# Two units of an output projection and two of a feed-forward stage in token halves, without GpSimd

## The reference, cut to what matters

```python
x = x + rms_norm_2(merged @ w_out[l], norm_mix_post_g[l])   # output projection, its norm, residual
h = rms_norm_2(x, norm_ffn_pre_g[l])                        # norm ahead of the third FFN
f = (jax.nn.silu(h @ w_gate[l]) * (h @ w_up[l])) @ w_down[l]
x = x + rms_norm_2(f, norm_ffn_post_g[l])
```

## Time and profile before

| what | us |
|---|---|
| median of 3 runs | 1896.39 |
| the three runs | 1894.55, 1896.39, 7628.95 |
| the profiled execution | 1894.26 |
| its span, first to last instruction | 1892.5 |
| TensorE busy | 1870.1 (99%) |
| VectorE, ScalarE, GpSimd busy | 926.3 (49%), 717.8 (38%), 164.4 (9%) |
| granted TensorE clock, mean over the span | 0.997 of full |

### The profile page before, as it was taken

The page is one execution under the profiler, slowest core; times in us unless marked ns, Lnnn a source line. Parts: engine busy times, 40 slices in busy tenths (PEclk is TensorE's granted clock), DMA queues, the critical chain, the costliest instruction groups (busy, mean ns, idle before and its releaser), DMA issues.

```text
span 1892.5 us, 23419 instructions
## 1 busy us (share of the span) xinstructions
PE 1870.1 (99%) x9226; PEld 1527.5 (81%) x9226; DVE 926.3 (49%) x1202; ACT 717.8 (38%) x973; POOL 164.4 (9%) x141
## 2 busy tenths in 40 slices
PE   9999999999999999999999999999999899999998
PEld 7888888887779888888888888777888778888887
DVE  4444431456685655544443146654666364444323
ACT  6223222364534443432232134445664452232222
POOL 0000000125330200200000012110100030000000
PEclk9999999999999999999999999999999999999999
DMA  6343332232214223333332224333422323433322
GB/s 179 89 109 90 90 110 89 101 100 91 68 47 154 89 90 100 101 89 95 104 89 97 103 69 135 114 100 95 126 78 90 89 67 89 110 89 91 109 89 78
DMA packets 214304, 184.15 MB, mean 97 GB/s; under 512 B 7685, under 2 KB 192090, under 8 KB 214234
## 3 DMA queue, kind: packets, MB, share of 16 engines
q1 hardware_dynamic: 213536, 183.13, 31.8%
q10 hardware_dynamic: 698, 0.05, 0.0%
HBM read 172.67 MB, written 2.10 MB: 92 GB/s over the span
## 4 chain that ended last, share of the span: by engine, by line
PE 94%; DVE 3%; ACT 1%; issue 1%; POOL 0%; DMA 0%; SPq 0%; DVEq 0%; ACTq 0%
PE bank L545 26%; PE bank L547 26%; PE bank L546 26%; PE bank L725 6%; PE bank L593 2%; PE bank L595 2%; PE bank L594 2%; PE bank L1023 1%; DVE n_lo L1648 1%; PE bank L1007 1%; ACT w_hi L1123 1%; PE bank L993 1%; PE bank L992 0%; DVE x L2184 0%; PE bank L609 0%
## 5 line engine op out<-in xcount | busy, mean ns | idle before, releaser
L1639 DVE TENSOR_TENSOR w_lo<-w_raw,w_hi 128x2048 fp32r<-128x2048 f32 x160 | 368.2, 2301 | 716.4 <-ACT w_hi L1123 716.2
L545 PE MATMUL bank<-n_hi,w_hi 128*128 128x512 f32 x1760 | 702.2, 399 | 11.0 <-DVE n_lo L1648 9.7
L547 PE MATMUL bank<-n_hi,w_lo 128*128 128x512 f32 x1760 | 687.1, 390 | 0.0
L546 PE MATMUL bank<-n_lo,w_hi 128*128 128x512 f32 x1760 | 686.8, 390 | 0.0
L1123 ACT CAST w_hi<-w_raw 128x2048 fp32r<-128x2048 f32 x160 | 305.5, 1909 | 601.6 <-PE bank L547 508.6
L545 PEld LDWEIGHTS bank<-n_hi,w_hi 128*128 128x128 f32 x1760 | 331.1, 188 | 84.0 <-issue 11.5
L547 PEld LDWEIGHTS bank<-n_hi,w_lo 128*128 128x128 f32 x1760 | 330.9, 188 | 70.1
L546 PEld LDWEIGHTS bank<-n_lo,w_hi 128*128 128x128 f32 x1760 | 331.4, 188 | 68.3 <-issue 3.4
L481 POOL TENSOR_TENSOR sum_squares<-sum_squares,sq 128x512 f32<-128x512 f32 x35 | 61.6, 1760 | 900.2 <-ACT sq L1138 896.9
L545 PE MATMUL bank<-h_hi,w_hi 128*128 (+1 forms) x352 | 137.2, 390 | 0.2
L547 PE MATMUL bank<-h_hi,w_lo 128*128 (+1 forms) x352 | 136.9, 389 | 0.0
(11 more groups left out here) (302 smaller groups left out, 1828.8 us busy)
## 6 DMA issues: line engine op xcount, KB each, us to landing
w_raw<-in_w_in SPq DMA_DIRECT2D x68, 512.0 KB, 4.6
w_raw<-in_ffn_down SPq DMA_DIRECT2D x44, 512.0 KB, 4.0
w_raw<-in_ffn_gate SPq DMA_DIRECT2D x43, 512.0 KB, 4.0
w_raw<-in_ffn_up SPq DMA_DIRECT2D x43, 512.0 KB, 5.2
w_raw<-in_w_gate SPq DMA_DIRECT2D x22, 512.0 KB, 4.0
w_raw<-in_w_up SPq DMA_DIRECT2D x22, 512.0 KB, 5.2
w_raw<-in_w_down SPq DMA_DIRECT2D x22, 512.0 KB, 3.9
w_raw<-in_w_kv_mem SPq DMA_DIRECT2D x16, 512.0 KB, 4.5
```

Of the source, the lines that this page charges most:

```text
L545: pe.matmul(acc, w_hi, x_hi, start=start, stop=False)
L546: pe.matmul(acc, w_hi, x_lo, start=False, stop=False)
L547: return pe.matmul(acc, w_lo, x_hi, start=False, stop=stop)
L1639: dve.tensor_tensor(wlo[par][:, :], raw[par][:, :], whi[par][:, :].bitcast(F32), ALU.subtract).then_inc(w_lo_ready, 1)
```

## The change

Five things are done.

1. U_OUT2+2 and U_OUT2+3 are each done in two passes over 256 of the 512 tokens (`dense_half`): first half of unit 2, first half of unit 3 (banks 0 to 3), then second half of unit 2 and of unit 3 (banks 4 to 7). The sum over partitions and the root are done for each half (`sum_post`, `post_root`).
2. The first two units of the third FFN are done in token halves (`half_units`): both units on the first 256 tokens, then both on the second. The sums and turns hang in between as hooks.
3. `tmp`, `x`, `n_hi` and `n_lo` of this stage are made in halves of 256 tokens.
4. GpSimd does nothing more there: its products go to VectorE, and so do its sums of squares, which VectorE now adds after the second half from a new tile `lastsq` (8 chunks; it lies over tiles that are free at that time).
5. The preload of ScalarE's table ahead of the last root falls away, and the first two copies of turned tokens (`copy_turned`) come ahead of unit 2's cast.

The core of the diff, PE first, then ScalarE, then VectorE:

```diff
-            pool.wait_ge(rstd_ready, R_POST2 + 1)
-            for c in range(1, C, 2):
...
-            add_squares(S_FFN3, range(3, C))
+            def dense_half(u, first_bank, half, xh, xl, hooks=None):
+                unit_split(u)
+                s = u % 2
+                for m in range(2):
+                    for k in range(C):
+                        w0 = k * 256 + m * P
+                        mm = products(bank[first_bank + m][:, HALF[0]], whi[s][:, w0:w0 + P], wlo[s][:, w0:w0 + P],
+                                      xh[:, k, HALF[half]], xl[:, k, HALF[half]], k == 0, k == C - 1)
+                        if k == C - 1:
+                            mm.then_inc(unit_done if m and half else half_done, 1)
+                        if hooks and C * m + k in hooks:
+                            hooks[C * m + k]()
+                def half_units():
+                    hooks = {(0, 0, 1): lambda: sum_post(1), (0, 1, 4): turn_first, (1, 1, 2): sum_last, (1, 1, 6): turn_rest}
+                    for half in range(2):
+                        for jj in range(2):
+                            u = base + jj
+                            par = u % 2
+                            unit_split(u)
+                            for k in range(C):
+                                if jj == 0:
+                                    pe.wait_ge(n_ready, C * index + half_count(half, k))
+                                for g in range(2):
+                                    w0 = (g * C + k) * P
+                                    mm = products(bank[2 * jj + g][:, HALF[half]], whi[par][:, w0:w0 + P],
+                                                  wlo[par][:, w0:w0 + P], nhi[:, k, HALF[half]], nlo[:, k, HALF[half]],
+                                                  k == 0, k == C - 1)
...
+            def sum_post(half):
+                pe.wait_ge(sq_added, post_add(C - 2, half))
+                acc = bank[4 * half][:, HALF[0]]
+                pe.matmul(acc, ones[:, :], sumsq[:, HALF[half]], start=True, stop=False)
+                pe.wait_ge(sq_ready, post_square(C - 1, half))
+                pe.matmul(acc, ones[:, :], sq[(C - 1) % 2][:, HALF[half]], start=False, stop=True).then_inc(sq_summed, 1)
+            for j in (2, 3):
+                dense_half(U_OUT2 + j, 2 * j, 1, mhi, mlo, {2: lambda: sum_post(0)} if j == 2 else None)
...
+            for c in range(4, C):
+                post_chunk(c, 0)
+            post_root(0)
+            post_chunk(4, 1)
+            for c in range(3):
+                last_hi(c, 0)
+            split_unit(U_FFN3)
+            post_chunk(5, 1)
+            for c in (3, 4):
+                last_hi(c, 0)
+            post_chunk(6, 1)
+            last_hi(5, 0)
+            post_chunk(7, 1)
+            split_unit(U_FFN3 + 1)
+            last_hi(6, 0)
+            last_hi(7, 0)
+            post_root(1)
+            for c in range(C):
+                last_hi(c, 1)
+                act.activation(lastsq[:, c, :], x[:, c, :], ACT.Square).then_inc(sq_ready, 1)
+            act.wait_ge(xt_turned, 2)
+            for i in range(2):
+                copy_turned(i, x_tok_a)
             split_unit(U_FFN3 + 2)
-            inverse_root(S_FFN3, R_FFN3)
...
+            def post_half(half, between):
+                cols = HALF[half]
+                dve.wait_ge(rstd_ready, R_POST2 + half + 1)
+                post_scaled(0, half)
+                for c in range(C):
+                    if c < C - 1:
+                        post_scaled(c + 1, half)
+                    dve.wait_ge(scaled, half_count(half, c))
+                    dve.tensor_tensor(x[:, c, cols], tmp[c % 2][:, cols], x[:, c, cols], ALU.add).then_inc(x_ready, 1)
+                    if c:
+                        last_lo(c - 1, half)
+                    between(c)
+                last_lo(C - 1, half)
+            def between_first(c):
+                if c == 1:
+                    post_sum(4, 1)
+                if c == 3:
+                    split_unit(U_FFN3)
+                    post_sum(5, 1)
+                if c == 5:
+                    post_sum(6, 1)
...
+            for c in (4, 5, 6):
+                post_sum(c, 0)
+            post_half(0, between_first)
             split_unit(U_FFN3 + 1)
+            post_half(1, lambda c: None)
+            for c in range(1, C):
...
+                dve.tensor_tensor(sumsq[:, :], lastsq[:, 0, :] if c == 1 else sumsq[:, :], lastsq[:, c, :], ALU.add).then_inc(sq_added, 1)
             ffn_steps(2, U_FFN3, R_FFN3)
```

More of the change, by code:

```diff
@@ L645, in gate_up, with turn_first, sum_last, turn_rest @@
                             hooks[k]()
-                def turn_middle():
-                    pe.wait_ge(rstd_ready, R_FFN3 + 1)
[L649 to L654, removed]
+                def turn_first():
+                    pe.wait_ge(rstd_ready, R_POST2B + 1)
+                    turn_x(0, 4)
+                    turn_x(1, 6)
+                def sum_last():
+                    pe.wait_ge(xt_ready, 4)
+                    pe.wait_ge(sq_added, last_add(C - 1))
+                    pe.matmul(bank[7][:, :], ones[:, :], sumsq[:, :], start=True, stop=True).then_inc(sq_summed, 1)
+                def turn_rest():
+                    pe.wait_ge(rstd_ready, R_FFN3 + 1)
+                    turn_x(2, 4)
+                    turn_x(3, 6)
+                def half_units():
[13 more added lines that the diff above has]
+                                                  k == 0, k == C - 1)
+                                if half and k == C - 1:
+                                    mm.then_inc(unit_done, 1)
+                                if (half, jj, k) in hooks:
+                                    hooks[half, jj, k]()
                 if f == 0:
@@ L1167, in inverse_root, with copy_turned @@
                 act.activation(rstd[:, :], sumsq[:, :], ACT.Exp, scale=-0.5).then_inc(rstd_ready, 1)
+            def copy_turned(i, dst):
+                for half in range(2):
+                    act.copy(dst[:, i % 2, T * half:T * half + T],
+                             bank[4 + 2 * (i % 2) + half][:, :]).then_inc(xt_ready, 1)
             def ffn_steps(f, base):
@@ L1186, in gate_up @@
                     act.copy(dst, tmp[jj][:, :]).then_inc(h_hi_ready, 1)
[L1188 to L1191, removed]
                 b = base + 2
                 if f == 2:
-                    act.wait_ge(xt_turned, 1)
-                    copy_turned(0, x_tok_a)
+                    inverse_root(S_FFN3, R_FFN3, load=False)
                 for j in range(2):
@@ L1609, in _, with post_chunk @@
-            inverse_root(S_POST2, R_POST2, 6, load=False)
-            feed(N_FFN3, X_MIX2, "norm_ffn_pre_g_2", S_FFN3, U_FFN3 + 1, lag=3)
+            def post_chunk(c, half=None):
+                if half is None:
+                    act.wait_ge(unit_done, U_OUT2 + c // 2 + 1)
+                    b, cols, src = c, slice(0, T), slice(0, T)
+                else:
+                    if half and c % 2:
+                        act.wait_ge(unit_done, U_OUT2 + c // 2 + 1)
+                    else:
+                        act.wait_ge(half_done, c - 3 if not half else 5 + (c - 4) // 2)
+                    b, cols, src = c if half else c - 4, HALF[half], HALF[0]
+                if c >= 3:
+                    act.wait_ge(sq_added, post_add(c - 2, half if half and c >= 6 else 0))
+                dst = (sq[c % 2] if c else sumsq)[:, cols]
+                act.activation(dst, bank[b][:, src], ACT.Square, scale=0.5).then_inc(sq_ready, 1)
+                act.activation(ypost[:, c, cols], bank[b][:, src], ACT.Copy, scale=small[:, PG + c:PG + c + 1]).then_inc(ypost_ready, 1)
@@ new lines, in _ @@
+            for j in range(2):
+                split_unit(U_OUT2 + j + 2)
+                for c in (2 * j, 2 * j + 1):
+                    post_chunk(c)
+            for c in range(4, C):
[10 more added lines that the diff above has]
+            last_hi(5, 0)
@@ L2166, in _ @@
             split_unit(U_OUT2 + 1)
[L2168 to L2186, removed]
```

90 lines of the change are left out of this document (54 added, 36 removed).

## The result

| | median us | runs | ratio to before, fast runs (95%) |
|---|---|---|---|
| before | 1894.75 | 5 (1894.29 up, one of 7628.95) | |
| changed | 1885.02 | 5 (1883.09 to 1886.40) | 0.9945 (0.9932 to 0.9959) |
| changed, again | 1883.71 | 5 (1883.38 to 1885.37) | 0.9939 (0.9925 to 0.9952) |

The ratio is that of the fast executions, and the one of 7628.95 us is not among them. The profiled execution took 1883.09 us with a span of 1881.3.

A forecast was written before the change was run, and what follows sets the result against it. TensorE bounds, busy 1870.1 of 1892.5 us. In the stage 46.0 + 1.7 + 0.9 + 3.5 + 0.9 = 53.0 for 63.4, -10.4; 1883.9 or 1886.0 by starting run, taken as 1885.2; range 1881.5 to 1891.5.

The forecast's parts named there:

- Half-width matmuls: Four units' 192 matmuls become 384 of 256 columns at 0.1198 us: 46.0 against 43.5, +2.5 us on TensorE's path.
- The order on TensorE: U_OUT2+2 to FFN unit 2, laid out in time: waits of 0.4 and 0.5 us, end at 1537.8, -10.4 us.
- GpSimd taken out: VectorE takes about 8 us more work, but its instructions lose 7 us of excess; covered by TensorE's second halves.
- The clock: TensorE's low clock from 1514.85 to 1520.83 goes, as no wait exceeds 0.5 us: 2.8 us back, inside the sum.
- Rival 1: VectorE's first pass is slower than said: gain only 3 to 8 us, 1886 to 1893; chance 0.15.
- Rival 2: Weight loads of 0.192 us set the pace of half-width matmuls: +30 instead of +2.5, end at 1913; chance 0.03.
- Rival 3: The clock falls in another place where a wait grows: price 2.8 us, 1888 or more; chance 0.04.
- Rival 4: More gain: no new waits, half-width starts exactly half of 0.2267 apart; 13.8 us at most, 1882.4; chance 0.06.
- Rival 5: GpSimd's work lay under waits the halves remove anyway; time stays near 1885; no chance of its own given.

The follow-up runs named there:

- e4: Kernel before with the 20 gate units in the third FFN's loop done in two passes of 256 tokens; 1909.57 us, ratio 1.0072.
- e2: Kernel before, full width, with GpSimd's products and adds of the stage moved to VectorE; stage 60.11 us, median 1890.92 us, ratio 0.9978.
- e3: Changed kernel plus a chain of eleven GpSimd multiplies of 128x512 on a scratch tile; stage 61.70 us, median 1892.14 us, ratio 0.9982.
- e7: Changed kernel plus one 128x512 VectorE instruction after each chunk of VectorE's second pass (4.8 us more); stage 56.87 us, ratio 0.9968.
- e1: Kernel before plus 50 matmuls on constants between the post sum and the third FFN; stage 64.3 us, median 1895.12 us, ratio 1.0000.
- e6: Changed kernel plus one 128x512 VectorE instruction after each chunk of VectorE's first pass (4.8 us more); stage 55.68 us, ratio 0.9954.
- e8: Changed kernel with the second half's sum and the first two turns moved to other places on TensorE; stage 52.27 us, median 1883.13 us, ratio 0.9931.
- e9: Changed kernel with the output projection back to full width and only the FFN's two units in halves; stage 58.83 us, ratio 0.9970.
- e10: Kernel before plus 25 matmuls on constants ahead of the third FFN; stage 64.3 us, median 1895.59 us, ratio 1.0004.
- the last version: Changed kernel with two hooks moved on TensorE, run again beside the changed kernel; stage 52.25 us, median 1882.52 us, ratio 0.9930.

## Why the prediction was right

Forecast: 1885.2 us, 10.4 us in the stage, against 1885.02 (1883.71 the second time) and 10.3. Point by point:

- *Half-width matmuls.* 0.1198 was taken from the memory keys; the stage shows 0.1199 and the loop of e4 0.12 over 1920 of them. The term of 2.5 us holds. One reading beside it was wrong. Solving the two spacings (0.1198 for 256 columns, 0.2267 for 512) gives a fixed part of 0.013 us a matmul; the 6 ns named in the prediction are what a half-width matmul costs over half a full one. By the formula of the Trainium skill ("TensorE: Matmul & The Clock Gate", Back-to-back issue gap) e4 would have cost an estimated 2.5 us; it cost 13.6, so the measurement decides. The same section of the Trainium skill says that the formula is for matmuls apart from a stream of weight loads, and that within such a stream it is too low for small ones and too high for large ones. The trace agrees for 256 columns (0.1198 us against 0.109) but not for 512 (0.2267 against 0.216).
- *The order on TensorE.* The waits were to be 0.4 and 0.5, for the second sum and for `w_lo`. The list of waits has only 0.34 for `w_lo`, but the starts show both: 0.43 us ahead of the second sum where 0.12 is normal, with another 0.1 inside it, and 0.62 ahead of 1515.41. The stage is 1.0 us longer than its work (53.10 against 52.1) where 0.9 was forecast. Unit 2 at 1537.8 forecast, measured 1537.10 with a start 0.79 earlier: 0.1 us off. VectorE's passes end at 1513.1 and 1524.5, where 1513.8 and 1525.1 were forecast: 0.7 earlier, nearly that shift.
- *GpSimd taken out.* The reason was right: the long instructions were contention (e2, e3), and VectorE could carry the work. The prediction counts 12 half products as new; they stand for four full ones of 0.60 dropped and 16 half ones of 0.34 added, so the new work was reckoned at 7.2 us and not 8, which the forecast does not use. The adds were mis-sized: 0.80 apart, not 0.60, which cost nothing in the changed kernel and showed only in e7.
- *The clock.* Here the account was right as an account and wrong as a cause. I counted 13.8 us in which TensorE did not work at full pace, and 2.8 of them as the low clock's. That the clock stays up in the changed kernel came true. But e1 shows that lifting the clock alone gives nothing in the kernel before, because the low parts of the chunks set the pace. The 2.8 us come back only because the halves take away the wait in which they lay.
- *The rivals.* Rival 1 (VectorE's first pass) did not occur, but e6 shows that it is where the risk was: 4.8 us more on VectorE cost 2.6. Rival 2 fell with e4. Rival 3, a low clock in another place, did not occur in the changed kernel, but e3 shows its kind: after a wait of 6.5 us the low clock cost 2.0 to 2.8 us, near the price of 2.8. Rival 4's kind of gain exists, 0.8 us, by moving the hooks (e8); its figure of 1882.4 follows from no starting point given there (1885.2 less the further 3.4 is 1881.8). Rival 5, that taking GpSimd's work out adds nothing once the halves are there, fell with e3: with such work back the stage is 8.6 us longer.
- *The whole time.* Part of the agreement is luck: the place where the stage begins moves by 3.6 us between the profiled executions, as told below. The stage is the better measure, but there is some luck in it too. The sum starts from the 63.40 us of one execution; from the 64.24 of e4 it would be a gain of 11.1. The range's lower end, 1881.5, was called the end of the possible losses; from the profiled 1894.26 that end is 1880.5.

## What to carry to other kernels

When one engine is the bound and idles only at a norm between two products, split the tokens, so that the first half's sum, root and scaling run beside the second half of the product before: this gave 5.7 of 10.3 us here, and halves on the far side alone only 1.3. Lay the new lists of all engines out in time from measured rows before building; instructions that depend on the one before need their own price (0.80 against 0.60 us here). Do not count a low clock as a cost before asking whether a later wait hides it: in the kernel before one did, in e3 none did and it cost 2 us or more. And do not give GpSimd work that reads SBUF while VectorE is the chain that others wait for, even when nobody waits for GpSimd.

## What the runs showed of the hardware

**A low clock after a wait.** Slow matmuls followed after TensorE had idled 6.3 us (before), 5.4 (e2), 6.5 (e3) and 3.8 (e9), but not after 2.1 (e6). The mean granted clock from 1505 to 1530 was 0.86, 0.93, 0.80, 0.93 and 1.00 in that order. In e10 they followed after the idle 3.3 us ahead of 1527.50. In the kernel before, e2 and e9 a further wait of TensorE for VectorE comes behind the slow matmuls and hides them, at least in part; in e3 none comes.

**Scatter from the first 40 us.** The same code up to 1480 ran with different granted clocks at its start. The stretches 0 to 40 us of the changed kernel, of its repetition, and of the last version:

```profile
0.00:40.00 40.00, 37.44 (x171) 30.97 (x172) 21.02 (x38) 27.73 (x40) 3.35 (x12) 1.00 0.65 185
```

```profile
0.00:40.00 40.00, 36.53 (x161) 29.58 (x162) 18.79 (x36) 27.25 (x39) 3.35 (x12) 0.96 0.66 185
```

```profile
0.00:40.00 40.00, 36.26 (x155) 29.35 (x156) 17.73 (x35) 27.14 (x39) 3.35 (x12) 0.91 0.66 185
```

At 1.00, 0.96 and 0.91 the stage began at 1484.00, 1486.31 and 1487.57, and the spans were 1881.3, 1883.6 and 1884.1 us. From 40 to 1480 TensorE was busy 1437.7 us in each. All fourteen profiled executions fit: the five with 1.00 in that stretch began the stage at 1484.0 to 1484.9, the eight with 0.96 at 1485.9 to 1486.6, the one with 0.91 at 1487.57. So the 2 to 3 us by which executions differ go with the clock at the start; that the clock is their whole cause was not tested.
